# Eight places for expert weights used in turn over rounds of four written-out steps, in a one-core transformer block

## The chip, the core and the metric

The kernel runs on one core of a Trainium2 chip, in one launch. The core has five engines that run side by side, each with its own instruction stream: TensorE (PE, matrix products), VectorE (DVE), ScalarE (ACT), GpSimd (POOL) and SyncE (SP), which here only issues transfers from memory. They are ordered by semaphores alone. The metric is the time of one execution in microseconds on the device. Lower is better.

## What is computed

Two transformer blocks follow each other on 256 tokens of 1024 features, all in float32. The first has a mixer (stick-breaking attention and a gated recurrence), a layer norm, and a mixture of 32 experts of which each token takes 4. The second has a mixer (a gated convolution and a state-space scan) and a convolution-gated feed-forward part. The change touches the stage of the experts. What an expert computes on the rows that chose it, from the reference:

```python
def expert_block(args):
    xblk, e = args
    hcat = xblk @ w_up[e] + b_up[e]
    x_glu = jnp.minimum(hcat[:, 0::2], SWIGLU_LIMIT)
    x_lin = jnp.clip(hcat[:, 1::2], -SWIGLU_LIMIT, SWIGLU_LIMIT)
    act = x_glu * jax.nn.sigmoid(SWIGLU_ALPHA * x_glu) * (x_lin + 1.0)
    return act @ w_down[e] + b_down[e]
```

`w_up[e]` is 1024 x 2048 and `w_down[e]` 1024 x 1024. The results are weighted by the router's gates and summed per token; a scaled residual and a layer norm follow.

## The kernel before

The program has two blocks of instruction streams with a barrier between them. The first is `mixer1`: the first mixer, its layer norm and the router. The second holds `experts`, `mixer2` and `ffn`, one after the other on each engine.

**Routing.** The router gives each expert up to 64 rows (`SLOTS`) in a step. A step is one expert with at most 64 of its tokens; if an expert had more, a second pass over all 32 experts would follow. The number of steps, 32 times the passes, is worked out on DVE at the end of `mixer1` (L771) and written to `s.n_steps`; every engine reads it into a register (`n_steps`, L1017). Here one pass is enough, so there are 32 steps.

**Weights.** The weights of one expert come as six units of 2 MiB (`EXPERT_UNITS`): units 0 to 3 are quarters of `w_up`, units 4 and 5 halves of `w_down`. There are six places in on-chip memory for them, one for each unit (`s.expert_units`): unit 0 lies in two thirds of the ring `s.raw` through which both mixers and the feed-forward part load their weights, units 1 to 3 in `expert_weights`, units 4 and 5 in `expert_weights_late`. The late ones lie over tensors of `mixer1`: the fourth's place over its branch outputs, the fifth's over `x_hi` and `x_lo`. Behind these, in the same memory, come `m1_w_hi` and `m1_w_lo`, the split weights that the mixer's products read.

**Order of the loads.** SP issues all of them on one queue, in program order. The units of expert 0 are issued by the end of `mixer1` (L332 to L341), each after the wait that says that its place is free; the last, unit 5, waits for the last product of `mixer1` (`gemm_done` at `NW + 12`). The loads of all later experts stand in a loop in `experts.sync` (L1023): the load of unit u of the next expert waits until TensorE has finished with unit u of this one (`unit_mm`). After the loop SP waits for `up_out` and loads two pieces of the second mixer's weights into the ring (`load_first`).

**TensorE's step.** The loop at L1206 has one step for each turn: the up-projection, 32 matmuls over units 0 to 3 (`up_part`, L1182), turns of the result (`turn`, L1189), the gathering of the next step's rows (L1153, L1161), the scattering of the last step's result (L1172, L1166), and the down-projection, 16 matmuls over units 4 and 5 (`down_part`, L1198). Ahead of each unit it waits for that unit's `full` semaphore. Each float32 matmul of the program stands as two records in the trace. `unit_mm` is raised as TensorE has finished with a unit. DVE and ACT have loops of their own, one step a turn.

## Time and profile before

| | us |
|---|---|
| three runs | 1785.86, 1786.74, 1788.35 |
| median | 1786.74 |
| the profiled execution | 1784.85 |
| its span in the trace | 1783.1 |

| stretch of the span, us | what runs |
|---|---|
| 0 to 273 | `mixer1` and the router, up to the barrier |
| 273 to 1206 | the experts, 32 steps |
| 1206 to 1783 | `mixer2` and `ffn` |

The profile is one execution, 1.75 us longer on the device than its span and 1.89 us under the median. Its page gives busy times and 40 slices of the span; the chain of work that ended last tells what set the end; the windows table gives busy time, granted clock and DMA for any stretch.

### The profile page before, as it was taken

Reading aid. Unit: us, or ns where it says so; the run is one execution under the profiler, and the core shown is the slowest. Engines: PE = TensorE matmul, PEld = TensorE weight load, DVE = VectorE, ACT = ScalarE, POOL = GpSimd, SP = SyncE. Lnnn points to the kernel's source line nnn. Section 1 sums busy time; section 2 is a strip of 40 time slices with the busy share of each in tenths; the row PEclk is TensorE's granted clock in tenths of the full one; section 3 lists DMA queues with packets and bytes.
Section 4 is the critical chain, followed back from the end, with each engine's and each line's share of the span. In section 5 each row is a group of like instructions: output and inputs, shape, how many; then the busy total and the mean of one; then the engine's idle time right before and its main releaser. Section 6 shows DMA issues by size and latency. Waiting matters only on the chain.

```text
span 1783.1 us, 24595 instructions
## 1 busy us (share of the span) xinstructions
PE 1681.0 (94%) x10035; PEld 1067.9 (60%) x10035; DVE 691.1 (39%) x1192; ACT 618.4 (35%) x849; POOL 72.6 (4%) x53
## 2 busy tenths in 40 slices
PE   6989988999999999999999999999999999999998
PEld 6989873333333333333333333337999988989996
DVE  3568652212121211112121212125488665566654
ACT  3734421112121212111111212125465578465434
POOL 2003100000000000000000000000020022100000
PEclk9989988999999999999999999999999999999999
DMA  8443376999999999999999999993655444455552
GB/s 256 141 142 119 119 306 262 432 428 431 429 431 429 432 428 432 428 432 430 431 430 430 429 430 430 430 413 114 193 175 179 142 142 142 164 175 176 181 189 95
DMA packets 150274, 534.90 MB, mean 300 GB/s; under 512 B 5523, under 2 KB 103955, under 8 KB 117456
## 3 DMA queue, kind: packets, MB, share of 16 engines
q1 hardware_dynamic: 148976, 531.06, 75.5%
q0 software_dynamic: 1248, 3.14, 0.6%
q8 instruction: 36, 0.59, 0.1%
q14 instruction: 14, 0.11, 0.0%
HBM read 533.13 MB, written 1.05 MB: 300 GB/s over the span
## 4 chain that ended last, share of the span: by engine, by line
PE 43%; DMA 37%; ACT 3%; DVE 1%; issue 1%; SPq 0%; DVEq 0%; ACTq 0%
DMA expert_weights<-in_expert_w_up_dram 37%; PE bank L1182 10%; PE bank L123 9%; PE bank L124 9%; PE bank L125 9%; PE bank L1198 2%; PE bank L1153 1%; ACT back_w_hi L107 1%; PE bank L1172 1%; PE bank L1189 0%; DVE back_w_lo L111 0%; ACT b_c_v L1441 0%; PE bank L1728 0%; DVE b_c_v L1596 0%; PE bank L1718 0%
## 5 line engine op out<-in xcount | busy, mean ns | idle before, releaser
L1182 PE MATMUL bank<-expert_weights,x_gathered 128*64 128x512 f32 x1536 | 346.5, 596 | 46.9 <-DMA expert_weights<-in_expert_w_up_dram 46.9
L1118 DVE TENSOR_TENSOR pre_act<-bank,bias_now 128x512 f32<-128x512 f32 x64 | 44.0, 688 | 691.6 <-PE bank L1189 691.6
L1182 PEld LDWEIGHTS bank<-expert_weights,x_gathered 128*64 128x64 f32 x1536 | 105.7, 137 | 282.3 <-issue 182.0
L111 DVE TENSOR_TENSOR back_w_lo<-raw_weights,back_w_hi 128x2048 fp32r<-128x2048 f32 x90 | 206.7, 2299 | 88.8 <-ACT back_w_hi L107 87.7
L1198 PE MATMUL bank<-expert_weights_late,activations 128*64 128x512 f32 x1024 | 226.8, 596 | 0.0
L107 ACT ACTIVATE back_w_hi<-raw_weights 128x2048 fp32r<-128x2048 f32 x90 | 170.2, 1892 | 97.9 <-PE bank L125 97.9
L123 PE MATMUL bank<-u_hi,back_w_hi 128*128 128x256 f32 x704 | 201.4, 286 | 0.2 <-DVE u_lo L1520 0.2
L124 PE MATMUL bank<-u_lo,back_w_hi 128*128 128x256 f32 x704 | 199.4, 283 | 0.0
L125 PE MATMUL bank<-u_hi,back_w_lo 128*128 128x256 f32 x704 | 199.4, 283 | 0.0
L1058 ACT ACTIVATE up_rows<-bank 128x512 f32<-128x512 f32 x32 | 19.1, 597 | 385.4 <-PE bank L1182 385.4
L1198 PEld LDWEIGHTS bank<-expert_weights_late,activations 128*64 128x64 f32 x1024 | 70.8, 137 | 131.7 <-issue 127.8
L123 PEld LDWEIGHTS bank<-u_hi,back_w_hi 128*128 128x128 f32 x704 | 135.1, 192 | 2.4 <-issue 0.7
L125 PEld LDWEIGHTS bank<-u_hi,back_w_lo 128*128 128x128 f32 x704 | 135.2, 192 | 0.0
L124 PEld LDWEIGHTS bank<-u_lo,back_w_hi 128*128 128x128 f32 x704 | 135.2, 192 | 0.0
L1182 PE MATMUL bank<-raw_weights,x_gathered 128*64 128x512 f32 x512 | 117.8, 603 | 0.8 <-ACT x_gathered L1046 0.8
L123 PE MATMUL bank<-v_hi,back_w_hi 128*128 128x256 f32 x352 | 100.0, 284 | 0.2 <-DVE v_lo L1941 0.2
L125 PE MATMUL bank<-v_hi,back_w_lo 128*128 128x256 f32 x352 | 99.7, 283 | 0.0
L124 PE MATMUL bank<-v_lo,back_w_hi 128*128 128x256 f32 x352 | 99.7, 283 | 0.0
L111 DVE TENSOR_TENSOR m_w_lo<-raw_weights,m_w_hi 128x2048 fp32r<-128x2048 f32 x30 | 72.8, 2430 | 55.9 <-ACT m_w_hi L107 55.8
L123 PE MATMUL bank<-x_hi,m_w_hi 128*128 128x256 f32 x288 | 84.9, 295 | 6.6 <-DVE m_w_lo L111 6.6
L1068 ACT ACTIVATE y_rows<-bank 128x512 f32<-128x512 f32 x32 | 19.1, 597 | 205.8 <-PE bank L1198 205.8
L124 PE MATMUL bank<-x_lo,m_w_hi 128*128 128x256 f32 x288 | 83.5, 290 | 0.0
(387 smaller groups left out, 2568.4 us busy)
## 6 DMA issues: line engine op xcount, KB each, us to landing
expert_weights<-in_expert_w_up_dram SPq DMA_DIRECT2D x96, 2048.0 KB, 25.3
expert_weights_late<-in_expert_w_down_dram SPq DMA_DIRECT2D x64, 2048.0 KB, 20.5
raw_weights<-in_expert_w_up_dram SPq DMA_DIRECT2D x32, 2048.0 KB, 23.3
raw_weights<-in_w_in_dram SPq DMA_DIRECT2D x62, 1024.0 KB, 5.3
raw_weights<-in_w_up_dram SPq DMA_DIRECT2D x22, 1024.0 KB, 5.1
raw_weights<-in_w_down_dram SPq DMA_DIRECT2D x10, 1024.0 KB, 5.0
raw_weights<-in_w_s_out_dram SPq DMA_DIRECT2D x8, 1024.0 KB, 4.9
raw_weights<-in_w_out_dram SPq DMA_DIRECT2D x4, 1024.0 KB, 5.2
```

The lines of the kernel that those rows point to most:

```text
L107: act.activation(self.w_hi[:, s, 0:size], self.s.raw[:, s, 0:size], ACT.Copy).then_inc(self.hi_done, 1)
L111: dve.tensor_tensor(self.w_lo[:, s, 0:size], self.s.raw[:, s, 0:size], self.w_hi[:, s, 0:size].bitcast(FP32), ALU.subtract).then_inc(self. ...
L123: pe.matmul(out, lhsT=ah, rhs=bh, start=start, stop=False, skip_group_check=shared)
L124: pe.matmul(out, lhsT=ah, rhs=bl, start=False, stop=False, skip_group_check=shared)
L125: return pe.matmul(out, lhsT=al, rhs=bh, start=False, stop=stop, skip_group_check=shared)
L1058: act.activation(up_rows[:, 0, :], U[0][:, :], ACT.Copy).then_inc(up_out, 1)
L1068: act.activation(y_rows[:, :], U[0][:, :], ACT.Copy, scale=0.5).then_inc(y_out, 1)
L1118: dve.tensor_tensor(both.rearrange("p g k n -> p (g k) n").rearrange("p a (h n) -> p a h n", h=2), TB[b][:, :].rearrange("p (a h n) -> p a ...
L1153: m = pe.matmul(TB[0][rows[c], :], lhsT=onehot[:, t, :], rhs=s.h[:, t, 512 * c:512 * c + 512], start=(t == 0), stop=(t == 1))
L1172: m = pe.matmul(s.bank[ACC + 2 * t + c][:, :], lhsT=scatter[rows[c], P * t:P * t + P], rhs=y_rows[rows[c], :], start=False, stop=True, ski ...
L1182: m = pe.matmul(U[b][rows[half], :], lhsT=xg[:, 2 * u + a, :], rhs=w[:, a, 512 * c:512 * c + 512], start=(first and a == 0), stop=(last an ...
L1198: m = pe.matmul(U[0][rows[c], :], lhsT=act_t[:, b, g, half, :], rhs=w[:, half, g, 512 * c:512 * c + 512], start=(b + half + g == 0), stop= ...
```

## The change

The six places become eight (`PLACES`), and a unit no longer has a place of its own. The units of all experts are numbered on: unit j of a round goes to place j modulo 8. A round (`ROUND`) is four steps, 24 units, so that 24 is a multiple of 8 and every unit of a round has the same place in each round.

- `mixer1.sync` issues units 5, 6 and 7 after the last product of `mixer1`, where it issued unit 5: units 6 and 7 are units 0 and 1 of expert 1. Their two places of 16 KB per partition lie behind the two late ones, over `m1_w_hi` and the first part of `m1_w_lo`.
- `experts.sync` issues the rest of the first round's loads outside a loop, and in the loop 24 loads per turn. Each waits for the end of the work on the unit eight before it, where it waited for the unit six before.
- After the loop SP waits for `y_out` at n, where it waited for `up_out` at 2n. The ring's place 0 is last used by the next to last step.
- TensorE's loop has four steps written out per turn and turns a quarter as often. The work of a step is the same. The loops of ACT and DVE stay as they are.
- DVE writes a second number, the number of rounds, beside `n_steps`; SP and TensorE read it as well.

The label under which the change goes also names the second mixer's small products; the diff has no line in `mixer2`.

```diff
--- before.py
+++ after.py
@@ -26,7 +26,7 @@
 SB_HEADS, SB_DIM = 8, 64
 HG_HEADS, HG_DIM = 4, 128
 N_EXPERTS, TOP_K, SLOTS = 32, 4, 64
-EXPERT_UNITS = 6
+EXPERT_UNITS, PLACES, ROUND = 6, 8, 4
 PASSES = T // SLOTS
 DEEPNORM_ALPHA = 2.0 ** 0.25
 LN_EPS, HG_EPS, RMS_EPS = 1e-5, 1e-6, 1e-5
@@ -330,14 +330,15 @@
                 sp.dma_start(ln_b, A["ln1_b"][0].partition_broadcast(P)).then_inc(ln_loaded, 16)
 
                 sp.wait_ge(hg_done, 4)
-                for u in (1, 2, 3):
-                    s.load_expert_unit(sp, u, 0)
+                for j in (1, 2, 3):
+                    s.load_expert_unit(sp, j, 0)
                 sp.wait_ge(st.gemm_done, NW + 8)
                 s.load_expert_unit(sp, 4, 0)
                 sp.wait_ge(st.lo_done, N_UNITS - 1)
                 s.load_expert_unit(sp, 0, 0)
                 sp.wait_ge(st.gemm_done, NW + 12)
-                s.load_expert_unit(sp, 5, 0)
+                for j in range(5, PLACES):
+                    s.load_expert_unit(sp, j, j // EXPERT_UNITS)
 
             @block.gpsimd
             def _(pool):
@@ -769,6 +770,7 @@
                 step(dve.tensor_tensor(cnt[:, 15:16], cnt[:, 14:15], cnt[:, 13:14], ALU.add))
                 own.wait()
                 step(dve.tensor_scalar(s.n_steps[0:1, 0:1], cnt[0:1, 15:16], float(N_EXPERTS), None, op0=ALU.add))
+                step(dve.tensor_scalar(s.n_steps[0:1, 1:2], cnt[0:1, 15:16], float(N_EXPERTS), 1.0 / ROUND, op0=ALU.add, op1=ALU.mult))
                 own.wait()
 
             @block.tensor
@@ -987,9 +989,9 @@
             sems.append(nc.alloc_semaphore(name))
             return sems[-1]
 
-        sb("late_units_place", [P, 2, KD * 512])
+        sb("late_units_place", [P, PLACES - 4, KD * 512])
         bias_t = s.bias_t
-        weights, full, load = s.expert_units, s.expert_full, s.load_expert_unit
+        places, full, load = s.expert_places, s.expert_full, s.load_expert_unit
         xg, g_rows = sb("x_gathered", [P, KD, SLOTS]), sb("gathered_rows", [P, 512])
         up_rows = sb("up_rows", [P, 2, 512])
         y_rows = sb("y_rows", [P, 512])
@@ -1017,16 +1019,21 @@
         def n_steps(eng):
             return eng.value_load(s.n_steps[0:1, 0:1], min_val=N_EXPERTS, max_val=PASSES * N_EXPERTS)
 
+        def n_rounds(eng):
+            return eng.value_load(s.n_steps[0:1, 1:2], min_val=N_EXPERTS // ROUND, max_val=PASSES * N_EXPERTS // ROUND)
+
         def sync(sp):
             s.load_first(sp, 2)
             n = n_steps(sp)
-            with sp.Fori(0, n - 1) as i:
-                for u in range(UNITS):
-                    sp.wait_ge(unit_mm, i * UNITS + u + 1)
-                    load(sp, u, (i + 1) % N_EXPERTS)
-
-
-            sp.wait_ge(up_out, n * 2)
+            rounds = n_rounds(sp)
+            for j in range(PLACES, ROUND * UNITS):
+                sp.wait_ge(unit_mm, j - PLACES + 1)
+                load(sp, j, j // UNITS)
+            with sp.Fori(0, rounds - 1) as q:
+                for j in range(ROUND * UNITS):
+                    sp.wait_ge(unit_mm, q * (ROUND * UNITS) + (ROUND * UNITS + j - PLACES + 1))
+                    load(sp, j, (q * ROUND + (ROUND + j // UNITS)) % N_EXPERTS)
+            sp.wait_ge(y_out, n)
             for i in range(2):
                 s.load_first(sp, i)
 
@@ -1173,9 +1180,13 @@
                                   start=False, stop=True, skip_group_check=True)
                 return m
 
-            def up_part(u, b, first, last):
-
-                w = weights[u].rearrange("p (a n) -> p a n", a=2)
+            def unit_loaded(q, j):
+                pe.wait_ge(full[j % PLACES], (q * (ROUND * UNITS // PLACES) + j // PLACES + 1) * 16)
+
+            def up_part(j, b, first, last):
+
+                u = j % UNITS
+                w = places[j % PLACES].rearrange("p (a n) -> p a n", a=2)
                 for a in range(2):
                     for half in range(2):
                         c = 2 * b + half
@@ -1189,9 +1200,9 @@
                     m = pe.transpose(TB[b][:, P * gk:P * gk + P], up_rows[:, b, gk:512:4], C("identity"))
                 m.then_inc(turned, 1)
 
-            def down_part(b):
-
-                w = weights[4 + b].rearrange("p (c g n) -> p c g n", c=2, g=2)
+            def down_part(j, b):
+
+                w = places[j % PLACES].rearrange("p (c g n) -> p c g n", c=2, g=2)
                 for half in range(2):
                     for g in range(2):
                         for c in range(2):
@@ -1203,19 +1214,22 @@
             turn_gather(0)
             pe.wait_ge(cleared, 1)
             n = n_steps(pe)
-            with pe.Fori(0, n) as i:
+
+            def step(q, r):
+                i = q * ROUND + r
+                j = UNITS * r
                 pe.wait_ge(gather_out, i + 1)
-                pe.wait_ge(full[0], (i + 1) * 16)
-                up_part(0, 1, True, False)
+                unit_loaded(q, j)
+                up_part(j, 1, True, False)
                 pe.wait_ge(y_out, i + 1)
-                up_part(0, 0, True, False).then_inc(unit_mm, 1)
+                up_part(j, 0, True, False).then_inc(unit_mm, 1)
                 for u in range(1, 3):
-                    pe.wait_ge(full[u], (i + 1) * 16)
-                    up_part(u, 0, False, False)
-                    up_part(u, 1, False, False).then_inc(unit_mm, 1)
-                pe.wait_ge(full[3], (i + 1) * 16)
-                up_part(3, 0, False, True).then_inc(first_mm, 1)
-                up_part(3, 1, False, True).then_inc(unit_mm, 1)
+                    unit_loaded(q, j + u)
+                    up_part(j + u, 0, False, False)
+                    up_part(j + u, 1, False, False).then_inc(unit_mm, 1)
+                unit_loaded(q, j + 3)
+                up_part(j + 3, 0, False, True).then_inc(first_mm, 1)
+                up_part(j + 3, 1, False, True).then_inc(unit_mm, 1)
                 pe.wait_ge(up_out, i * 2 + 1)
                 turn(0)
                 pe.wait_ge(up_out, i * 2 + 2)
@@ -1229,9 +1243,13 @@
                 turn_scatter()
                 turn_gather(i + 1)
                 for b in range(2):
-                    pe.wait_ge(full[4 + b], (i + 1) * 16)
+                    unit_loaded(q, j + 4 + b)
                     pe.wait_ge(act_ready, i * 2 + b + 1)
-                    down_part(b)
+                    down_part(j + 4 + b, b)
+
+            with pe.Fori(0, n_rounds(pe)) as q:
+                for r in range(ROUND):
+                    step(q, r)
             pe.wait_ge(y_out, n + 1)
             pe.wait_ge(scatter_out, n)
             for t in range(TT):
@@ -2041,7 +2059,7 @@
         s.eps_ln, s.eps_hg = s.eps[:, 0:1], s.eps[:, 1:2]
         s.gate = sb("expert_gates", [P, TT, N_EXPERTS])
         s.slot = sb("expert_slots", [P, TT, PASSES * N_EXPERTS + 1])
-        s.n_steps = sb("n_steps", [1, 1], INT32)
+        s.n_steps = sb("n_steps", [1, 2], INT32)
 
         s.row_map = {"norm_mix_w_2": (0, 32, 8), "ssd_norm_w_2": (0, 40, 16), "conv_a_w_2": (0, 56, 24),
                      "ssd_conv_b_2": (0, 80, 24), "hgrn_lb_logits": (0, 104, 8), "hgrn_norm_g": (0, 112, 4),
@@ -2055,16 +2073,17 @@
         s.col = lambda name, i: colrange(name, i, 1)
         s.out = out
         s.raw_full = {name: [nc.alloc_semaphore(f"{name}_raw_full{i}") for i in range(RING)] for name in ("m1", "back")}
-        s.expert_full = [nc.alloc_semaphore(f"expert_unit{u}_full") for u in range(EXPERT_UNITS)]
-
-        def load_expert_unit(sp, u, e):
-
+        s.expert_full = [nc.alloc_semaphore(f"expert_place{p}_full") for p in range(PLACES)]
+
+        def load_expert_unit(sp, j, e):
+
+            u, place, full = j % EXPERT_UNITS, s.expert_places[j % PLACES], s.expert_full[j % PLACES]
             if u < 4:
                 w = A["expert_w_up"][0].rearrange("e (u p a) n -> e u p (a n)", p=P, a=2)[bass.ds(e, 1), u, :, :]
-                sp.dma_start(s.expert_units[u], w.rearrange("o p n -> (o p) n")).then_inc(s.expert_full[u], 16)
+                sp.dma_start(place, w.rearrange("o p n -> (o p) n")).then_inc(full, 16)
             else:
                 w = A["expert_w_down"][0].rearrange("e (c p g) n -> e p c (g n)", p=P, g=2)[bass.ds(e, 1), :, 2 * (u - 4):2 * (u - 4) + 2, :]
-                sp.dma_start(s.expert_units[u].rearrange("p (c n) -> p c n", c=2), w.rearrange("o p c n -> (o p) c n")).then_inc(s.expert_full[u], 16)
+                sp.dma_start(place.rearrange("p (c n) -> p c n", c=2), w.rearrange("o p c n -> (o p) c n")).then_inc(full, 16)
         s.load_expert_unit = load_expert_unit
 
         def load_first(sp, i):
@@ -2078,10 +2097,10 @@
                 nc.sbuf_tensor("bias_t", [P, N_EXPERTS, 4, 4], FP32) as s.bias_t, \
                 nc.sbuf_tensor("b_down", [N_EXPERTS, D], FP32) as s.b_down:
 
-            s.expert_units = [s.raw[:, 0:2, :].rearrange("p a n -> p (a n)")] + [s.expert_weights[:, u, :] for u in range(3)]
-
-            with nc.sbuf_tensor("expert_weights_late", [P, 2, KD * 512], FP32) as late:
-                s.expert_units += [late[:, i, :] for i in range(2)]
+            s.expert_places = [s.raw[:, 0:2, :].rearrange("p a n -> p (a n)")] + [s.expert_weights[:, u, :] for u in range(3)]
+
+            with nc.sbuf_tensor("expert_weights_late", [P, PLACES - 4, KD * 512], FP32) as late:
+                s.expert_places += [late[:, i, :] for i in range(PLACES - 4)]
             mixer1(nc, A, s)
             s.h_ready = nc.alloc_semaphore("m2_h_ready")
             expert_programs = experts(nc, A, s)
```

## Rows read from the trace of the kernel before

**Rows 1.** The page: span, TensorE's line, and DMA share in 40 slices.
```profile
span 1783.1 us, 24595 instructions
PE 1681.0 (94%) x10035; PEld 1067.9 (60%) x10035; DVE 691.1 (39%) x1192; ACT 618.4 (35%) x849; POOL 72.6 (4%) x53
...
DMA  8443376999999999999999999993655444455552
```

**Rows 2.** Windows table: stretch, busy us (records) per engine, clock, DMA share, GB/s.
```profile
258.00:260.00 2.00, 2.00 (x11) 2.00 (x11) 0.00 (x0) 0.00 (x0) 0.00 (x0) 0.50 0.37 156
260.00:273.00 13.00, 11.70 (x32) 5.65 (x31) 6.23 (x48) 0.91 (x3) 0.00 (x0) 0.76 0.00 0
...
300.00:350.00 50.00, 49.89 (x236) 17.84 (x234) 8.78 (x33) 9.55 (x16) 0.00 (x0) 1.00 1.00 422
350.00:500.00 150.00, 145.99 (x684) 53.35 (x682) 31.62 (x108) 30.84 (x52) 0.00 (x0) 1.00 1.01 430
500.00:1000.00 500.00, 467.19 (x2158) 165.20 (x2156) 89.58 (x306) 93.24 (x153) 0.00 (x0) 1.00 1.01 430
...
100.00:200.00 100.00, 90.36 (x705) 87.80 (x703) 71.81 (x75) 39.38 (x39) 20.84 (x7) 0.95 0.38 123
```

**Rows 3.** Chain that ended last, in time order: start us, us, what.
```profile
310.75 13.73 PE bank L1182 x64
...
337.75 13.73 PE bank L1182 x64
...
432.64 25.10 DMA expert_weights<-in_expert_w_up_dram
...
487.00 3.68 PE bank L1182 x16
...
1163.60 25.34 DMA expert_weights<-in_expert_w_up_dram
1188.98 3.65 PE bank L1182 x16
```

**Rows 4.** Timeline of SP's queue: start us, us, what it issues.
```profile
230.68 0.33 SPq L2064 DMA_DIRECT2D raw_weights<-in_expert_w_up_dram  x1
246.46 0.38 SPq L2067 DMA_DIRECT2D expert_weights_late<-in_expert_w_down_dram  x1
273.28 0.38 SPq L2074 DMA_DIRECT2D raw_weights<-in_w_in_dram  x1
287.45 0.36 SPq L2064 DMA_DIRECT2D raw_weights<-in_expert_w_up_dram  x1
...
1193.30 1.61 SPq L2074 DMA_DIRECT2D raw_weights<-in_w_in_dram  x2
```

**Rows 5.** Timeline around the first step's start; idle before and releaser in brackets.
```profile
279.16 1.12 PE L1161 MATMUL bank<-shared_constants,gathered_rows 128*128 128x128 f32 x4 [0.70 <-ACT gathered_rows L1042]
280.33 0.60 ACT L1046 ACTIVATE x_gathered<-bank 128x512 f32<-128x512 f32 x1 [1.22 <-PE bank L1161]
...
281.06 6.14 PE L1182 MATMUL bank<-raw_weights,x_gathered 128*64 128x512 f32 x16 [0.77 <-ACT x_gathered L1046]
```

**Rows 6.** Timeline of TensorE around a loop's end early on, and after the last step.
```profile
330.66 7.09 PE L1198 MATMUL bank<-expert_weights_late,activations 128*64 128x512 f32 x32
337.58 3.60 PE L1182 MATMUL bank<-raw_weights,x_gathered 128*64 128x512 f32 x16
...
1198.80 7.09 PE L1198 MATMUL bank<-expert_weights_late,activations 128*64 128x512 f32 x32
1206.59 1.99 PE L1172 MATMUL bank<-y_rows,scatter 64*128 64x512 f32 x8 [0.69 <-ACT y_rows L1068]
```

**Rows 7.** DMA queues (packets, MB, share): whole span, 100 to 200, 400 to 1150 us.
```profile
q8 instruction: 36, 0.59, 0.1%
...
q8 instruction: 6, 0.10, 0.4%
...
q1 hardware_dynamic: 28752, 322.75, 100.9%
```

## The prediction

> **What bounds the kernel now.** I read the page first. TensorE is busy 94% of the span, and the DMA line of the 40 slices is at 9 from slice 8 to slice 26, nearly the whole stage of the experts [rows 1]. Two resources look full, so the question is which one sets the pace, and the windows table and the chain answer it. The windows show 430 GB/s at a share of 1.01 from 350 to 1000 us, while TensorE is busy 467 of 500 us [rows 2]: the transfers have no gap, TensorE has. The chain shows it in time. Early on it runs through TensorE's work alone, one step every 337.75 - 310.75 = 27.0 us [rows 3]. From 432 us on it is a pattern of one expert transfer of 25.3 us and 3.68 us of matmuls, 26 times, up to the last step [rows 3]. The matmuls after the wait start at 487.00 and, 24 steps later, at 1188.98: 701.98 / 24 = 29.25 us a step, which at 430 GB/s is 12.58 MB, six units of 2 MiB. A unit takes 29.25 / 6 = 4.875 us of the transfer engines. So from 432 us on the stage ends when its 192 units have come in, and TensorE, which could do a step in 27.0 us, waits for them.
>
> The next view is the timeline of SP's queue [rows 4], beside the windows around the start of the stage [rows 2]. The last unit of expert 0 is issued at 246.46 us, when the last product of the first mixer is done. The queue runs dry in the window 258 to 260 (156 GB/s instead of 430, so at about 258.7 us), and from 260 to 273 us nothing moves. Unit 0 of expert 1 is issued only at 287.45, when TensorE has finished with unit 0 of expert 0, because no place is free before. In this gap the transfers that set the end stand still.
>
> **What the change removes.** It gives the gap two units to carry. Places 6 and 7 lie over memory that the mixer's last product was the last to read, the same condition as for unit 5, so their loads are issued right behind it, at about 246.9 and 247.3 us (the issue of one takes 0.38 us [rows 4]). They start as the queue would run dry, at 258.7, and need 2 x 4.875 = 9.75 us: they are in at 268.5, before the piece of the second mixer's weights issued at 273.28 [rows 4]. So they displace nothing. Even if they came 5 us late there would be room, and more behind it.
>
> After that the transfers start again at 287.45 as before: unit 8 of the numbering waits for the first unit's matmuls, which end when they ended. Each further load waits for the unit eight before, and TensorE frees these at the old times, so the queue has its next transfer at the same moments as before, but each transfer is two units further on. The small loss at the start (422 GB/s from 300 to 350 us [rows 2]) stays. From then on the queue is never empty, before or after, since TensorE frees a step's places in 27.0 us and the transfers need 29.25 us to fill them. Every later landing is 9.75 us earlier. The steady pace does not change: eight places give a lead, not bandwidth.
>
> Does TensorE allow it? The first step starts at 281.06 [rows 5], the second at 310.75, and 31 steps of 27.0 us from there end at 1147.7. The last step's matmuls ended at 1205.9 (1198.80 + 7.09 [rows 6]) and would end at 1196.1. TensorE could be done 48 us sooner, so the stage stays bound by transfers to its end; only the part at TensorE's pace grows by 9.75 / 2.25 = some 4 steps. What follows the last landing (one unit of the up-projection, the tail of the step, scattering, layer norm) is the same work, so the whole second block starts 9.75 us earlier. Term: **-9.75 us**.
>
> **What it adds.**
> - *A second number to read, on TensorE ahead of its loop.* No row shows that read by itself. The one that is there lies between the end of the turns at 280.28 (279.16 + 1.12) and the first matmul at 281.06, so it costs at most 0.78 us, and it is covered now: the matmul follows the end of ACT's copy (280.33 + 0.60 = 280.93) by 0.13 us [rows 5]. A second one of at most 0.78 us could show between 0 and 0.78 us. A delay of the first matmul delays the first free place and with it every later transfer, so it counts in full. A gain is excluded, since nothing is taken away. I take 0.2, near the lower end, because the copy's 0.65 us cover most of one read.
> - *SP's second read, and sixteen loads outside the loop.* SP has from 273.7 to 287.45 with nothing to issue [rows 4]: 0, and below 1 us if that cover were gone. Later its queue is several transfers ahead, and an issue of 0.4 us stands against 4.875 us of transfer.
> - *DVE's second number.* One more operation of a few tenths of a us ahead of the barrier, beside TensorE's last matmuls of the router: 0, at most 0.2.
> - *Waits computed from a round's number.* They run in TensorE's sequencer while its matmuls run: at the end of a turn, matmuls of the next step follow those of this one without a gap (330.66 + 7.09 ends after 337.58 [rows 6]). Where they showed, they would cost slack of 2.25 us a step, not time: 0.
> - *The wait for `y_out` at n instead of `up_out` at 2n.* Nothing but the two pieces of ring weights stands behind it on SP. They were issued at 1193.30 [rows 4]; now they go out as soon as the step before last is done and queue behind the last unit. The second mixer's first matmuls come after the layer norm, later than both: 0.
>
> The sum is -9.75 + 0.2 = -9.55 us. Against the profiled execution's own 1784.85 us (span 1783.1) this gives 1775.3. The median of the three runs is 1.89 us above that execution, so the median after should be 1786.74 - 9.55 = **1777.2 us**.
>
> **Rival 1, slower: the round no longer stays with TensorE's sequencer.** Instructions come from memory too. I take queue 8 for TensorE's, as the one that moves with its record count: 36 packets, 0.59 MB, so 16.4 KB each [rows 7]. From 100 to 200 us TensorE executes 705 + 703 records, and 6 such packets come in [rows 2, 7]: some 235 records each. A step of the loop has (2158 + 2156) / (500 / 29.25) = 252 records, just over one packet, and in 750 us of looping not one instruction packet is seen [rows 7]: a loop body across at least two packets is kept. A round has 1008 records, 4.3 packets, and lies across five. If these are not all kept, each turn fetches them again: 7 turns after the first, 35 packets of 16.4 KB, 0.57 MB. Spread over the 16 engines that is 0.57 MB at 430 GB/s, 1.3 us, and 1778.5. But if they all fall to one transfer engine, that engine falls behind: at 430 / 16 = 26.9 GB/s a packet takes 0.61 us of it, 35 take 21.3 us, and since a unit is in only when the slowest engine has brought its part, the net is -9.55 + 21.3 = +11.8, **1798.5 us**. It decides from 16 packets on one engine, a little over two a turn. The wait at the loop's jump itself would be covered by matmuls already queued and by the slack of 9 us a round. For this rival speaks that the kept size is unknown above two packets; against it, that nothing says that it ends there.
>
> The Trainium skill speaks against the change here. Its page "Runtime: NRT & Kernel Launch", section "Instruction fetch mechanics", says that prefetch is sequential, and that a jump to a target outside the current two-page window forces a fetch before execution goes on; by that rule a round is fetched anew each turn, and the time is between the two ends of rival 1. The same section gives TensorE's buffer as 128 KiB, 2048 instructions; by that figure a round would be kept and the sum stands. The trace of before fits both.
>
> **Rival 2, no change: the early units buy nothing.** That is so if the lead is lost again, for instance if places were freed later and the queue ran dry once for 9.75 us after 287 us. Then the time is 1786.7. Against it: from 350 us to the end the DMA share is full [rows 2], and the releases come from a TensorE that is 2.25 us a step quicker.
>
> **How the numbers follow.** The forecast 0.77. Rival 1 spread over the engines 0.07 (1778.5, within the forecast's own range), on one engine 0.12. Rival 2, 0.04. The forecast's bounds: all added costs at 0 give 1777.0, all at their upper ends (-9.75 + 0.78 + 0.2 = -8.77) give 1778.0. The three runs spread by up to 1.6 us from their median, and a pace that differs by 0.1% over the 900 us of the stage is 0.9 us; I take 2.2 us of both to the low side and 2.5 to the high one. Range 1774.8 to 1780.5, with the spread form of rival 1 in it. It leaves out the slow case and rival 2, 0.16. This measurement can tell about 0.2%, 3.6 us, from no change: faster 0.84, within 0.04, slower 0.12.
>
> **What will show it.** In the profile after: two more loads issued near 247 us and a full DMA line up to 268 us; the chain at TensorE's pace up to some 530 us instead of 432; steps of 29.25 us after that; the last matmuls behind a transfer near 1179 us instead of 1188.98; from there the old distances. Instruction packets in the stage of the experts, and a step above 29.25 us, would show rival 1; the DMA share below 1.01 after 350 us, rival 2. The prediction is wrong if the pace of the transfers changes: each 0.1% of it is 0.9 us over the stage.

## The result and the profile after

| | before | after |
|---|---|---|
| median of the four runs each, taken together | 1786.35 us | 1775.08 us |
| lowest and highest | 1785.86, 1788.35 | 1773.32, 1776.96 |
| profiled execution, span | 1784.85, 1783.1 | 1773.35, 1771.6 |

The ratio is 0.9938, with a 95% interval of 0.9923 to 0.9952: 11.3 us less, between 9 and 14. The forecast was 1777.2, 9.55 us less. The sign, the place and the mechanism are as forecast; the four runs came out 2.1 us lower. They fell into two pairs, 1773.3 and 1776.9, and the profiled execution is of the faster one. A second set of six runs of the same kernel, below, has its median at 1778.0; all ten together have it at 1777.0.

The page of the changed kernel, as [rows 1]:

```profile
span 1771.6 us, 24443 instructions
PE 1676.1 (95%) x10035; PEld 1067.6 (60%) x10035; DVE 691.1 (39%) x1193; ACT 618.4 (35%) x849; POOL 72.6 (4%) x53
...
DMA  8443397999999999999999999984655444455552
...
q8 instruction: 39, 0.64, 0.1%
```

TensorE executes the same 10035 matmul records, DVE one operation more. In the DMA line the dip at the sixth and seventh digit, 3 7 before, is 9 7 now. Windows of the changed kernel (columns as in [rows 2]):

```profile
258.00:260.00 2.00, 2.00 (x11) 2.00 (x11) 0.00 (x0) 0.00 (x0) 0.00 (x0) 0.50 1.10 467
260.00:268.00 8.00, 7.88 (x24) 4.15 (x23) 4.53 (x32) 0.62 (x3) 0.00 (x0) 0.66 1.00 428
268.00:273.00 5.00, 3.70 (x8) 1.40 (x8) 1.76 (x18) 0.28 (x1) 0.00 (x0) 0.93 0.07 30
...
350.00:500.00 150.00, 149.34 (x703) 54.66 (x703) 31.18 (x108) 31.71 (x52) 0.00 (x0) 1.00 1.01 430
500.00:1000.00 500.00, 470.37 (x2176) 166.60 (x2174) 89.59 (x306) 93.25 (x153) 0.00 (x0) 1.00 1.01 430
```

The gap carries transfers up to just after 268 us and is empty again before 273; before, nothing moved from 260 to 273 [rows 2]. The pace afterwards is the old 430 GB/s. TensorE is busy 149.3 of the 150 us from 350 to 500, where it was busy 146.0: it begins to wait for transfers later than before. SP's queue shows the same, as [rows 4]:

```profile
246.38 0.38 SPq L2086 DMA_DIRECT2D expert_weights_late<-in_expert_w_down_dram  x1
246.80 0.95 SPq L2083 DMA_DIRECT2D expert_weights_late<-in_expert_w_up_dram  x2
273.15 0.38 SPq L2093 DMA_DIRECT2D raw_weights<-in_w_in_dram  x1
284.60 0.33 SPq L2083 DMA_DIRECT2D raw_weights<-in_expert_w_up_dram  x1
...
1165.74 17.60 SPq L2093 DMA_DIRECT2D raw_weights<-in_w_in_dram  x2
```

Two loads more behind the one at 246.38. But the load behind the first freed place goes out at 284.60, and in the kernel before it went out at 287.45. The forecast did not have this: it took this moment as unchanged. The chain of the changed kernel, as [rows 3]:

```profile
308.11 13.73 PE bank L1193 x64
...
335.11 13.73 PE bank L1193 x64
...
551.04 6.89 PE bank L1193 x32
558.08 34.33 DMA expert_weights_late<-in_expert_w_up_dram
592.46 3.65 PE bank L1193 x16
...
1142.91 34.49 DMA expert_weights_late<-in_expert_w_up_dram
1177.45 3.65 PE bank L1193 x16
```

The chain runs through TensorE's steps of 27.0 us up to 558 us instead of 432. The first wait of TensorE for a unit in this stretch stands in the timelines, of the kernel before and of the changed one:

```profile
452.88 3.65 PE L1182 MATMUL bank<-expert_weights,x_gathered 128*64 128x512 f32 x16 [0.30 <-DMA expert_weights<-in_expert_w_up_dram]
```

```profile
558.31 3.65 PE L1193 MATMUL bank<-expert_weights_late,x_gathered 128*64 128x512 f32 x16 [0.40 <-DMA expert_weights_late<-in_expert_w_up_dram]
```

It comes 105.4 us later: four steps of 27.0 us, less the 2.6 us by which the changed kernel's second step starts earlier (308.11 against 310.75). After that (1177.45 - 592.46) / 20 = 29.25 us a step, as before. The last expert's fourth unit sets TensorE free at 1177.45 instead of 1188.98: 11.53 us earlier, which is the whole gain of the span (1783.1 - 1771.6 = 11.5). A transfer in the chain is now 34.5 us long instead of 25.3: it is issued seven units ahead of its landing instead of five, and the step is the same 29.25 us. Behind it the old distances are kept: from there to the end of the span it is 1771.6 - 1177.45 = 594.15 us, and it was 1783.1 - 1188.98 = 594.12.

### The profile page after: what moved, and what is told of

The parts are those of the page before. It is cut to its first block, busy times and chain, and to the rows that moved or that the text cites. A ratio compares the mean times of both kernels' runs of the same rounds, so it can differ in the third digit from the quotient of the medians.

```text
span 1771.6 us, 24443 instructions
## 1 busy us (share of the span) xinstructions
PE 1676.1 (95%) x10035; PEld 1067.6 (60%) x10035; DVE 691.1 (39%) x1193; ACT 618.4 (35%) x849; POOL 72.6 (4%) x53
## 4 chain that ended last, share of the span: by engine, by line
PE 58%; DMA 21%; ACT 3%; DVE 1%; issue 1%; SPq 0%; DVEq 0%; ACTq 0%
PE bank L1193 14%; DMA expert_weights_late<-in_expert_w_up_dram 12%; DMA expert_weights<-in_expert_w_up_dram 10%; PE bank L123 9%; PE bank L125 9%; PE bank L124 9%; PE bank L1209 8%; PE bank L1160 3%; PE bank L1179 2%; PE bank L1200 2%; ACT back_w_hi L107 1%; PE bank L1168 1%; PE bank L1173 0%; DVE back_w_lo L111 0%; ACT b_c_v L1459 0%
## 5 line engine op out<-in xcount | busy, mean ns | idle before, releaser
L1193 PE MATMUL bank<-expert_weights_late,x_gathered 128*64 128x512 f32 x1024 | 228.1, 594 | 21.6 <-DMA expert_weights_late<-in_expert_w_up_dram 21.6
L1193 PE MATMUL bank<-expert_weights,x_gathered 128*64 128x512 f32 x768 | 171.3, 594 | 14.9 <-DMA expert_weights<-in_expert_w_up_dram 14.9
L1193 PEld LDWEIGHTS bank<-expert_weights_late,x_gathered 128*64 128x64 f32 x1024 | 71.4, 137 | 175.3 <-issue 129.7
L1193 PEld LDWEIGHTS bank<-expert_weights,x_gathered 128*64 128x64 f32 x768 | 53.9, 137 | 129.1 <-issue 97.2
L1209 PE MATMUL bank<-expert_weights_late,activations 128*64 128x512 f32 x512 | 113.4, 595 | 0.0
L1209 PE MATMUL bank<-expert_weights,activations 128*64 128x512 f32 x384 | 85.5, 594 | 0.0
```

Source lines behind the costliest of these rows:

```text
L1193: m = pe.matmul(U[b][rows[half], :], lhsT=xg[:, 2 * u + a, :], rhs=w[:, a, 512 * c:512 * c + 512], start=(first and a == 0), stop=(last an ...
L1209: m = pe.matmul(U[0][rows[c], :], lhsT=act_t[:, b, g, half, :], rhs=w[:, half, g, 512 * c:512 * c + 512], start=(b + half + g == 0), stop= ...
```

## What sets the end: the first freed place

To separate the parts I read three moments in each kernel: A, the issue of the ring load right behind the barrier; B, the issue of the load that waits for the first unit's matmuls; C, the start of the matmuls behind the last expert's fourth unit. From B on the queue always has a next load. Where the chain goes from transfer to transfer, a step takes 29.25 us, 4.875 us a unit, in the kernel before (487.00 to 1188.98, 24 steps) and in the changed one (592.46 to 1177.45, 20 steps). The last column is what C - B has beyond 4.875 us for each unit issued from B on: the time from an issue to its landing, and what is lost near the start, as from 305 to 310 us, where both kernels move some 370 GB/s instead of 430.

For the kernel before these are 273.28, 287.45 and 1188.98, with 184 units. For the changed one 273.15, 284.60 and 1177.45, with 182. In full:

| kernel | B - A | C - B | units | beyond 4.875 us a unit |
|---|---|---|---|---|
| before | 14.17 | 901.53 | 184 | 4.5 |
| changed | 11.45 | 892.85 | 182 | 5.6 |
| changed, second profile (e5) | 14.07 | 891.68 | 182 | 4.4 |
| six places, rounds of four (e1) | 14.01 | 903.14 | 184 | 6.1 |
| no early unit (e2) | 11.42 | 900.83 | 184 | 3.8 |
| one early unit (e3) | 14.08 | 896.02 | 183 | 3.9 |
| rounds of eight (e4) | 14.01 | 897.63 | 182 | **10.4** |
| rounds of sixteen (e9) | 14.07 | 897.46 | 182 | **10.2** |
| changed, filled (e6) | 11.96 | 892.82 | 182 | 5.6 |
| before, filled (e7) | 11.82 | 902.09 | 184 | 5.1 |
| nine places (e8) | 11.10 | 888.91 | 181 | 6.5 |
| nine places, filled (e10) | 11.61 | 888.24 | 181 | 5.9 |
| read later (e11) | 11.11 | 892.35 | 182 | 5.1 |
| old wait (e12) | 13.12 | 893.51 | 182 | 6.3 |

Three things can be read off. In all kernels but two the last column lies between 3.8 and 6.5 us. It differs by 1.2 us between two profiles of the same kernel, and what makes it differ was not found. Apart from it, C - B falls by one unit for each unit loaded early. And B - A has two sizes, about 14.1 and about 11.4 us, which do not go with the kernel: the changed kernel has shown both. (e12, at 13.12, lies between: there the clock was full at the turning and fell again during the first unit, to 0.67 on average from 280 to 284 us.) The 11.53 us between the two values of C are -2.85 (B), -9.75 (two units of 4.875) and +1.07 (the last column, 5.60 against 4.53).

A itself is no fixed moment either. It lies between 270.55 us (e12) and 276.97 (e5) in the 14 profiles, a wider spread than that of B - A, and it too is passed on to the end. The 5.2 us between the two profiles of the changed kernel are 3.8 from A, 2.6 from B - A and -1.2 from C - B. So which of these parted the four runs into two pairs is not shown.

What makes B - A differ is, for the most part, the clock granted to TensorE in the first step. Windows of the kernel before, of the changed kernel, and of its second profile, in which everything starts 3.8 us later:

```profile
281.00:284.00 3.00, 2.94 (x8) 1.01 (x10) 0.88 (x4) 1.28 (x1) 0.00 (x0) 0.50 0.10 24
284.00:288.00 4.00, 4.00 (x16) 1.16 (x14) 0.00 (x0) 0.00 (x0) 0.00 (x0) 0.74 0.00 0
```

```profile
281.00:284.00 3.00, 3.00 (x16) 1.04 (x18) 0.38 (x2) 1.00 (x1) 0.00 (x0) 1.00 0.06 13
284.00:288.00 4.00, 4.00 (x22) 1.44 (x20) 0.00 (x0) 0.00 (x0) 0.00 (x0) 1.00 0.61 180
```

```profile
284.00:288.00 4.00, 3.19 (x8) 1.03 (x10) 1.38 (x7) 1.88 (x2) 0.00 (x0) 0.50 0.28 99
```

The clock is at 0.50 of 2.4 GHz, 1.2 GHz, in the kernel before from 281 to 284 us and in the second profile of the changed kernel; in the first profile of the changed kernel it is at 2.4 GHz. The first unit's 16 matmul records start at 281.06 and take 6.14 us before [rows 5]; in the changed kernel's profile they start at 280.90 and take 3.65. What TensorE did just ahead of it is the same in all: eight records of gathering and four of turning, with idle time between. The turning took 1.12 us before and 0.74 in the changed kernel. In full, the 2.85 us of B are 0.13 (A), 0.38 (turning), 2.49 (the first unit) and 0.20 (SP's first load, which follows the start of the next unit's matmuls by 0.42 us in the old loop and by 0.22 when written out), less 0.35 by which the first matmul follows ACT's copy later; e11 below is about that. Why the clock was granted in one execution and not in the other stays open.

## The experiments

"Before" in the ratios is the kernel before, run on the same chip among them; its runs spread from 1779.0 to 1790.3 us over all batches, much wider than the three runs that were known, with medians from 1785.9 to 1786.5 in the three batches.

### e1: rounds without places

```diff
-EXPERT_UNITS, PLACES, ROUND = 6, 8, 4
+EXPERT_UNITS, PLACES, ROUND = 6, 6, 4
-            sp.wait_ge(y_out, n)
+            sp.wait_ge(up_out, n * 2)
```

> The whole change with six places instead of eight: rounds of four written-out steps, the second number and its reads, waits computed per round, no early units; the wait ahead of the ring loads is the old one, since with six places the last step uses place 0. If the lead in transfers is what gained, this is the time of the kernel before plus the read of 0 to 0.8 us: 1786 to 1787.5. If the written-out round or the loop gained, it is faster, down to 1775. In the trace: chain of transfers from about 432 us, no instruction packet between 400 and 1150 us.

Measured: ratio 1.0004 (0.9992 to 1.0017), 12 runs. The written-out round, the numbering and the second read together neither gain nor cost what can be told, 2 us or so. In 400 to 1150 us no instruction packet is seen.

### e2 and e3: the early units taken away, both or one

e2, and e3 with 7 in place of 6:

```diff
-                for j in range(5, PLACES):
+                for j in range(5, 6):
...
+            sp.wait_ge(unit_mm, 1)
+            for j in range(6, PLACES):
+                load(sp, j, j // UNITS)
             for j in range(PLACES, ROUND * UNITS):
```

> Eight places and rounds as in the changed kernel, but units 6 and 7 are issued only after TensorE has finished with unit 0, not at 247 us. If only the transfers put into the gap count, the eight places alone give nothing: 1786 to 1787.5, with the last expert's fourth unit landing near 1187 to 1189 us. If eight places help by themselves in the steady state, it stays near the changed kernel's 1775.

> Unit 6 is issued at 247 us, unit 7 only after TensorE has finished with unit 0. The theory of the lead says one unit of 4.875 us is missing: 4.9 us above the changed kernel and 4.9 below the one without early units, about 1781. If the gain comes from something that both share, it is at one of the two ends.

Measured: e2 1.0000 (0.9986 to 1.0014), e3 0.9973 (0.9961 to 0.9984), 12 runs each. With eight places and no early unit the gain is zero, to within 2.5 us; one early unit gives 0.27% of 1786, 4.8 us, as forecast 4.9. SP's queue in e2 and the end of its chain:

```profile
246.89 0.38 SPq L2089 DMA_DIRECT2D expert_weights_late<-in_expert_w_down_dram  x1
273.62 0.38 SPq L2096 DMA_DIRECT2D raw_weights<-in_w_in_dram  x1
285.04 0.82 SPq L2086 DMA_DIRECT2D expert_weights_late<-in_expert_w_up_dram  x2
285.91 0.43 SPq L2086 DMA_DIRECT2D raw_weights<-in_expert_w_up_dram  x1
```

```profile
1185.87 3.65 PE bank L1196 x16
```

Three loads go out at once at 285, but the transfers take up again only when the first place is free (B - A is 11.42 us, the changed kernel's 11.45), and nothing has been carried in the gap. The landing that I had put at 1187 to 1189 came at 1185.87, because B belongs to the full clock here. From 483.89 us on its chain takes 701.98 us for 24 steps, to the hundredth what the kernel before takes. So the places give nothing in the steady state, and deeper queueing does not speed the stage.

### e4 and e9: longer rounds

```diff
-EXPERT_UNITS, PLACES, ROUND = 6, 8, 4
+EXPERT_UNITS, PLACES, ROUND = 6, 8, 8
```

> Rounds of eight written-out steps instead of four, four turns, all else as changed: TensorE's loop body is some 2016 records, 8.6 instruction packets of 16.4 KB. If the kept size ends between 5 and 9 packets, each of the three later turns fetches 8 to 9 again, 24 to 27 packets, seen between 400 and 1150 us; on one transfer engine they cost up to 0.61 us each, +15 us, spread over all 1 us. If all is kept, the time is that of the changed kernel within 1 us and the window 400 to 1150 has at most the packets of the first turn.

Measured: 0.9978 (0.9965 to 0.9990), 12 runs; the changed kernel has 0.9947 in its second set, so 5 to 6 us of the gain are lost. The DMA queues from 400 to 1150 us, the first jump back in the chain, and two later moments of it:

```profile
q8 instruction: 32, 0.52, 0.2%
```

```profile
494.55 7.02 PE bank L1209 x32
501.57 2.09 issue
503.66 13.95 PE bank L1193 x64
```

```profile
597.49 3.65 PE bank L1193 x16
...
1186.76 3.65 PE bank L1193 x16
```

The instruction packets of rival 1 are there: 32, where I had put 24 to 27; three of them belong to the first turn. So the kept size ends between a round of four steps (4.3 packets) and one of eight (8.6). The first jump back leaves TensorE idle for 2.09 us. That idle time lies early on, where the transfers, not TensorE, will set the end, so it should not count. The chain shows where the time goes: from 597.49 to 1186.76 us are 20 steps, 589.27 us instead of 585.0. The 4.27 us are spread over the whole stretch, 0.15 to 0.8 us in every two steps (the two pairs with a jump in them have 0.8 and 0.4), and 24 packets come in there: 0.18 us a packet. e9 tells packets and jumps apart a second time:

```diff
-EXPERT_UNITS, PLACES, ROUND = 6, 8, 4
+EXPERT_UNITS, PLACES, ROUND = 6, 8, 16
```

> Rounds of sixteen written-out steps, two turns, else as the changed kernel. With rounds of eight 32 instruction packets came in between 400 and 1150 us, and the stage from the first freed place to the last expert's fourth unit took 897.6 us for 182 units, where the changed kernel took 892.85. Here about as many packets must come (every step's instructions are fetched once: 32 steps at 1.07 packets), but with one jump back instead of three. If the packets themselves cost transfer time, the stage takes 897 to 898 us again and the time stays some 4 to 5 us above the changed kernel. If the three jumps cost it (2 us each, with TensorE waiting at the jump), it takes 894 to 895 us.

Measured: 0.9970 (0.9958 to 0.9983), 12 runs, and

```profile
q8 instruction: 28, 0.46, 0.2%
```

```profile
1187.76 3.65 PE bank L1193 x16
```

C - B is 897.46 us against 897.63: one jump instead of three changes nothing, so the packets cost, not the jumps. Beside the two profiles of the changed kernel (892.85 and 891.68) it is 4.6 to 6.0 us more, for some 30 packets more, which agrees with 0.18 us a packet. This lies between my two ends, 0.04 (spread over 16 engines) and 0.61 (all on one). How the packets lie on the transfer engines is not in the trace, so why it is 0.18 stays open.

### e5, e6, e7: the clock of the first step

e5 is the changed kernel again. e6 adds to it, and e7 to the kernel before, one matmul ("filled" in the table):

```diff
+            pe.matmul(s.bank[0][:, :], lhsT=C("identity"), rhs=s.h[:, 0, 0:512], start=True, stop=True)
             gather(0)
```

> The changed kernel as it is, on the same chip as the three below, since its four runs fell into two groups, 1773.3 and 1776.9 us. My theory: the groups differ by the clock granted to TensorE in the first step; at 1.2 GHz the first unit's matmuls take 6.1 us instead of 3.4, so the first place comes free 2.85 us later and all later transfers with it. Expected: 1773 to 1778, a ratio to the kernel before of 0.994, two groups some 3 us apart.

> The changed kernel with one more 128x512 matmul (a value nobody reads, into bank 0) ahead of the first gathering, in the 2.6 us in which TensorE waits for the one-hot rows. If the clock theory holds and activity there brings the clock up earlier, the first step always runs at 2.4 GHz: the slow group vanishes, median 1773 to 1774.5, first freed place near 284.6 us. If it makes no difference to the clock: as the changed kernel.

> The same added matmul in the kernel before. By the clock theory its first freed place moves from 287.45 to about 284.6 us, and the time from 1786.3 to between 1783.4 and 1786.3, less than the changed kernel's gain in any case. If the clock has nothing to do with the end of the stage: 1786.3.

Measured: e5 0.9947 (0.9931 to 0.9963), runs from 1773.3 to 1781.0, median 1778.0; e6 0.9940 (0.9927 to 0.9954), runs from 1775.0 to 1778.6, five of the six within 0.9 us; e7 0.9997 (0.9985 to 1.0008). The six runs of e5 did not fall into two groups 3 us apart, as I had expected, and three of them lie above the range that I had put, one by 3 us. In e5's profile the first unit's matmuls ran at half clock (6.19 us), in those of e6, e7 and e10 at full clock (3.65 us). e6's windows and first rows:

```profile
277.00:281.00 4.00, 3.56 (x8) 0.64 (x8) 0.00 (x0) 0.40 (x1) 1.39 (x3) 0.52 1.07 349
281.00:284.00 3.00, 1.63 (x8) 0.91 (x10) 1.38 (x7) 1.86 (x3) 0.00 (x0) 1.00 0.64 242
```

```profile
274.90 2.05 PE L1213 MATMUL bank<-hidden,shared_constants 128*128 128x512 f32 x2 [1.17 <-PEq L974]
276.87 3.68 PE L1160 MATMUL bank<-hidden,onehot 128*64 128x512 f32 x8
```

The added matmul takes 2.05 us at half clock and ends as the gathering starts, 0.5 us later than without it: ACT's copy ends 7.8 us after A, and 7.3 without it at full clock. B - A is 11.6 to 12.0 with it, in three profiles of three, and below 11.5 in four of the eleven without. The two sizes are shown, and that B moves C follows from the step of 29.25 us, which is the same in all of them. That the filling secures the full clock is likely, not shown: one profile each, and the times of e6 and e5, and of e7 and before, overlap within their intervals. I had put 1773 to 1774.5 on e6 and it has 1775.9; e7's 1785.5 lies in its range of 1783.4 to 1786.3, which held no change as well.

### e8 and e10: a ninth place

Nine places, rounds of three steps, and the last two steps behind the loop. The number of steps is fixed at 32; the second pass over the experts that a fuller expert would need is left out. Some small tensors move so that the room is free. SP and TensorE read one number again, and the wait ahead of the ring loads is the old one.

```diff
-EXPERT_UNITS, PLACES, ROUND = 6, 8, 4
+EXPERT_UNITS, PLACES, ROUND = 6, 9, 3
...
-            with pe.Fori(0, n_rounds(pe)) as q:
+            with pe.Fori(0, N_EXPERTS // ROUND) as q:
                 for r in range(ROUND):
                     step(q, r)
+            for r in range(2):
+                step(N_EXPERTS // ROUND, r)
```

> Nine places: a third early unit is issued at 247 us, rounds of three steps with nine places, and the last two steps written out behind the loop (the number of steps is fixed at 32, which these inputs need; a second pass of the experts is left out). By the theory of the lead each early unit is worth 4.875 us: 4.9 us below the changed kernel, 1770. The gap holds it: three units end at 273.4 us, when the ring load is issued, so 4.4 to 4.9. If another limit is reached at eight places, it equals the changed kernel.

> Nine places with the added matmul ahead of the first gathering (the number of steps is fixed at 32, a second pass is left out). The theory of the clock says that the slow mode of the first step is gone: 1769 to 1771 with a narrow spread, ratio 0.991 to 0.992. If the added matmul only costs its own time, it is 1 us slower than nine places alone, 1772.

Measured: e8 0.9914 (0.9901 to 0.9927), median 1771.06; e10 with the added matmul 0.9901 (0.9884 to 0.9918), median 1768.84, five runs within 2.5 us. In e8:

```profile
245.05 1.43 SPq L2087 DMA_DIRECT2D expert_weights_late<-in_expert_w_up_dram  x3
271.04 0.38 SPq L2097 DMA_DIRECT2D raw_weights<-in_w_in_dram  x1
282.14 0.33 SPq L2087 DMA_DIRECT2D raw_weights<-in_expert_w_up_dram  x1
```

```profile
1171.05 3.65 PE bank L1195 x16
```

Three loads go out at 245, and the last of them is in just as the ring load goes out. Against the changed kernel's second set (0.9947) the gain is 0.33%, 5.9 us, with 3 to 4 us of noise; one unit is 4.9, and one read less is up to 0.3. So the third early unit agrees with what the first two were worth. I had put 1770 on e8 and 1769 to 1771 on e10. These two are the fastest of the study, for inputs that need one pass.

### e11 and e12: the small terms

e11 moves `n = n_steps(pe)` behind TensorE's loop. e12:

```diff
-            sp.wait_ge(y_out, n)
+            sp.wait_ge(up_out, n * 2)
```

> The changed kernel with TensorE's read of the number of steps moved behind its loop, so one read is left ahead of it, as before the change. In the changed kernel the first matmul follows the end of ACT's copy by 0.48 us, in the kernel before by 0.13. If the second read costs this, the gap is 0.1 to 0.2 us again. No effect on the time that a single look could tell.

> The changed kernel with the old wait, both copies of the last step's up-projection, ahead of the two ring loads. They are issued some 16 to 27 us later than in the changed kernel, behind the last step's up-projection. If nothing depends on them, the distance from the last expert's fourth unit to the first matmul of the second mixer's projections stays at 31.46 us (1177.45 to 1208.91); if the earlier loads gained something, it is longer.

The start of the first step in the changed kernel, whose ACT copy is the releaser, and in e11:

```profile
280.90 3.65 PE L1193 MATMUL bank<-raw_weights,x_gathered 128*64 128x512 f32 x16 [1.12 <-ACT x_gathered L1053]
```

```profile
281.19 0.60 ACT L1053 ACTIVATE x_gathered<-bank 128x512 f32<-128x512 f32 x1 [0.84 <-PE bank L1168]
...
281.94 3.65 PE L1193 MATMUL bank<-raw_weights,x_gathered 128*64 128x512 f32 x16 [0.79 <-ACT x_gathered L1053]
```

In the changed kernel the copy ran from 279.82 to 280.42, so the matmul followed by 0.48 us; in e11 by 281.94 - 281.79 = 0.15. The second read costs 0.33 us there. But it does not always: in e5, at half clock, with both reads, the copy ends at 284.62 and the matmul follows by 0.19.

```profile
284.02 0.60 ACT L1053 ACTIVATE x_gathered<-bank 128x512 f32<-128x512 f32 x1 [1.22 <-PE bank L1168]
284.81 6.19 PE L1193 MATMUL bank<-raw_weights,x_gathered 128*64 128x512 f32 x16 [0.82 <-ACT x_gathered L1053]
```

The other profiles agree. With two reads the matmul follows the copy by 0.47 to 0.48 us where the turning ran at full clock (changed, e2, e6, e12) and by 0.14 to 0.19 where it ran at half clock (e1, e3, e4, e5, e9). With one read it is 0.13 to 0.15 at either clock (before, e7, e8, e10, e11). So at half clock the slower turning covers the second read. The single run of each, 1775.1 and 1774.3 us, says nothing more of the time.

In e12 the ring loads go out at 1181.51 instead of 1165.74. The first matmul of the second mixer's projections, and the 32 records ahead of it:

```profile
1204.22 5.46 PE L1698 MATMUL bank<-group_rstd,hidden 128*128 128x128 f32 x32 [2.10 <-DVE hidden L187]
1209.88 0.36 PE L123 MATMUL bank<-u_hi,back_w_hi 128*128 128x256 f32 x1 [0.20 <-DVE u_lo L1538]
```

From C that is 1209.88 - 1177.18 = 32.70 us, 1.24 more than the changed kernel's 31.46. It looks like a price of the old wait, but it is not: those 32 records took 5.46 us instead of 4.23, the clock's doing again (0.72 on average from 1204 to 1210 us; it was full in the changed kernel from 1204 to 1209). e11, which has the new wait, shows the same:

```profile
1205.02 5.47 PE L1698 MATMUL bank<-group_rstd,hidden 128*128 128x128 f32 x32 [2.10 <-DVE hidden L187]
1210.69 0.36 PE L123 MATMUL bank<-u_hi,back_w_hi 128*128 128x256 f32 x1 [0.20 <-DVE u_lo L1538]
```

1210.69 - 1177.98 = 32.71 us. At the same clock the two waits give the same distance: the new wait is worth nothing.

## Why the prediction was right

**What bounds the kernel.** Right. The stage ends with its transfers, from e2 and e3 and from the step of 29.25 us, which is the same in every kernel with rounds of up to four.

**Two units in the gap, -9.75 us.** Right in mechanism and size: nothing without early units (e2), 4.8 us for one (e3), 9.5 to 11.3 for two, and e8 agrees with the same again for a third. The pace did stay at 4.875 us a unit.

**"TensorE frees these at the old times".** This step failed for the execution compared. I read 287.45 from one profile and took it as a property of the kernel. B - A has two sizes that belong to the clock granted in the first step, 2.6 us apart in the changed kernel. The evidence was in [rows 5]: 6.14 us for 16 records that take 3.60 a step later [rows 6]. I should have asked what happens if they ran at full clock, and widened the range by that much downwards. The measured median, 1775.08, lies inside the range only by 0.3 us, and the faster pair of runs lies below it; that it fell inside is luck. So was the base: the three runs that I had spread by 2.5 us, and the same kernel later by 11. With the same B on both sides the traces give -9.75 + 1.07 = -8.7; the small loss at the start, which I had let stay, was 1.07 us larger in the profile after. e5's six runs give 0.53%, 9.5 us, and the median of all ten runs, 1777.0, is 0.2 us from the forecast.

**The read on TensorE, 0.2 us.** It is 0.33 us at full clock and nothing that shows at half clock, both inside the bounds of 0 to 0.78. I had counted ACT's copy, 0.65 us, as cover for most of it. What decides it is the turning ahead of the copy: 1.12 us of it, as in [rows 5], leave the cover, and 0.74 us do not.

**Waits, SP's loads, DVE's number, the hand-over: 0.** Right (e1: +0.04% with an interval of 0.13% to either side; e11 and e12 for the hand-over), but for a gain of 0.2 us that I had not counted: SP's first load comes sooner behind its wait when it is written out. The distance from C to the end of the span is the same to 0.03 us.

**The time at TensorE's pace: to some 530 us.** The four steps more were right: TensorE first waits for a unit at 558.31 us instead of 452.88. I had added them to the wrong moment, 432.64, which is the issue of the chain's first transfer and not its landing.

**Rival 1.** It did not happen with rounds of four: 39 instruction packets instead of 36, three more in the first turn, and none from 400 us on. It does with rounds of eight. So the rival was a real edge, one doubling away, and its price lies between the two ends: 0.18 us a packet. With that price even a refetching round of four would have come to -9.75 + 35 x 0.18 = -3.5 us, an estimate: faster and not slower. The rule of the Trainium skill (page "Runtime: NRT & Kernel Launch", section "Instruction fetch mechanics") that a jump out of a two-page window forces a fetch does not hold here for TensorE, which jumped back over 4.3 packets of 16.4 KB without one from 400 to 1150 us; the same section's buffer of 2048 instructions agrees with both runs, 1008 records kept and 2016 records plus the loop's own instructions not.

**Rival 2.** Ruled out; e2 is what it would have looked like.

## What to carry to other kernels

In a stage that ends with its transfers, more places give a lead, not a pace: count how many units fit into the time in which the queue stands dry before the stage, and expect that many unit times, here 4.9 us each. Writing out more steps to make the numbering come out even cost nothing with a loop body of 1008 records on TensorE and some 5 us with 2016; look for instruction packets inside the loop. And before a moment of one profile is taken as fixed, look at the granted clock there: if the work ahead of it ran at half clock, price the other case too.

## What the runs showed of the hardware

- TensorE's loop body of 1008 matmul and weight-load records (4.3 packets of 16.4 KB) was fetched once; one of 2016 records was fetched anew in each turn, 32 packets in 750 us, and cost some 5 us of a saturated transfer stream, 0.18 us a packet (4.27 us for 24 packets in e4). At the first jump back TensorE stood idle 2.09 us.
- The same instructions at the same point ran at 1.2 GHz in one execution and at 2.4 GHz in another, at two places: at the first expert step (2.6 us between two profiles of the changed kernel) and after the layer norm that follows the experts (1.23 us for 32 records). The kernel before spread over 11 us in its runs, which three runs had shown as 2.5.
- A second read of a number into a TensorE register delayed the first matmul by 0.33 us where the work ahead ran at full clock, and by nothing that shows where it ran at half clock.
- A stream of 2 MiB loads from one queue held 4.875 us a unit, 430 GB/s, with five, seven and eight units in flight (transfers of 25.3, 34.5 and 38.7 us in the chain).
